# Moving nine gate chunks from the FoX loops to the sliding-window loops, and interleaving the prelude, in a fp32 hybrid attention layer

## The reference

```python
h = rmsnorm(x, norm_mix_pre)
z = h @ w_in   # FoX q,k,v (8 heads x 64) | forget logits (8) | SWA q (8x64), k, v (2x64) | gates g_fox, g_swa (1024 each)
logf = log_sigmoid(fa + fox_f_bias); cum = cumsum(logf)
# FoX: softmax(q.k/8 + cum_t - cum_s, causal) @ v
# SWA: chunks of 64, window of 3 chunks, relative bias, a sink per head, 4 query heads for one key head
y = sigmoid(g_fox) * (o_fox @ w_proj_fox) + sigmoid(g_swa) * (o_swa @ w_proj_swa)
x = x + rmsnorm(y @ w_o)
x = x + rmsnorm(conv_ffn(rmsnorm(x)))
```

## Time and profile before

| | |
|---|---|
| median of 3 runs | 1807.31 us (1806.53 to 1807.37) |
| the profiled execution, its time | 1807.58 us |
| its span, first to last instruction | 1805.8 us |
| TensorE busy | 1632.6 us (90%), 9375 products |
| VectorE, GpSimd, ScalarE busy | 992.1, 577.5, 430.7 us |
| mean granted TensorE clock | 0.961 of 2.4 GHz |

### The profile page before, as it was taken

How to read it: one execution, slowest core, us unless ns; L and a number is a source line. 1 busy time by engine, 2 the same in 40 slices (tenths; PEclk the granted TensorE clock), 3 DMA queues, 4 the chain that set the end, 5 groups by cost and what they waited for, 6 DMA issues and landing times.

```text
span 1805.8 us, 24441 instructions
## 1 busy us (share of the span) xinstructions
PE 1632.6 (90%) x9375; PEld 1512.7 (84%) x9375; DVE 992.1 (55%) x1874; ACT 430.7 (24%) x913; POOL 577.5 (32%) x312
## 2 busy tenths in 40 slices
PE   2779999999888977777699999999999999999996
PEld 2679999998877976766688799999999999999995
DVE  3645665657743258484944456455454554454456
ACT  4113342434521125352232211001001011011012
POOL 3242132222111330100813244334324324434442
PEclk9989999999988988897899999999999999999999
DMA  5342222222133420002543111101111112111115
GB/s 153 36 107 65 70 80 60 76 68 63 37 101 111 156 64 22 27 24 74 183 153 106 65 48 47 47 27 55 46 35 58 46 35 58 46 35 49 44 46 97
DMA packets 129615, 122.89 MB, mean 68 GB/s; under 512 B 7453, under 2 KB 116377, under 8 KB 129537
## 3 DMA queue, kind: packets, MB, share of 16 engines
q1 hardware_dynamic: 92468, 67.29, 13.0%
q10 hardware_dynamic: 35869, 50.22, 9.1%
q0 software_dynamic: 1200, 4.33, 1.4%
HBM read 94.00 MB, written 27.92 MB: 68 GB/s over the span
## 4 chain that ended last, share of the span: by engine, by line
PE 82%; DVE 13%; DMA 2%; issue 1%; ACT 1%; POOL 1%; SPq 0%; ACTq 0%; POOLq 0%; DVEq 0%
PE bank L643 17%; PE bank L644 17%; PE bank L645 17%; PE bank L649 6%; PE bank L651 6%; PE bank L650 6%; PE bank L675 5%; PE bank L787 2%; DVE m L1905 1%; DVE kl L1585 1%; DVE ssb L1658 1%; PE bank L758 1%; DMA raw<-in_w_in 1%; DVE ssb L1642 1%; PE bank L757 1%
## 5 line engine op out<-in xcount | busy, mean ns | idle before, releaser
L541 POOL TENSOR_TENSOR ring_h<-raw,att 128x1024 fp32r<-128x1024 f32 x108 | 208.2, 1928 | 1073.1 <-PE bank L645 844.8
L643 PE MATMUL bank<-m_h,ring_h 128*128 128x352 f32 x1056 | 340.7, 323 | 0.7 <-DVE m_l L1479 0.7
L644 PE MATMUL bank<-m_l,ring_h 128*128 128x352 f32 x1056 | 338.6, 321 | 0.0
L645 PE MATMUL bank<-m_h,ring_l 128*128 128x352 f32 x1056 | 338.4, 320 | 0.0
L643 PE MATMUL bank<-ht_h,ring_h 128*128 128x352 f32 x840 | 281.8, 336 | 11.1 <-DVE kt L1550 10.4
L542 POOL TENSOR_TENSOR ring_l<-raw,ring_h 128x1024 fp32r<-128x1024 f32 x108 | 287.9, 2666 | 8.5
L644 PE MATMUL bank<-ht_l,ring_h 128*128 128x352 f32 x840 | 275.6, 328 | 0.0
L645 PE MATMUL bank<-ht_h,ring_l 128*128 128x352 f32 x840 | 275.5, 328 | 0.0
L643 PEld LDWEIGHTS bank<-m_h,ring_h 128*128 128x128 f32 x1056 | 198.1, 188 | 1.2 <-DVE m_l L1479 0.8
L644 PEld LDWEIGHTS bank<-m_l,ring_h 128*128 128x128 f32 x1056 | 198.4, 188 | 0.3
L645 PEld LDWEIGHTS bank<-m_h,ring_l 128*128 128x128 f32 x1056 | 198.0, 188 | 0.0
(11 more groups left out here) (281 smaller groups left out, 2692.1 us busy)
## 6 DMA issues: line engine op xcount, KB each, us to landing
raw<-in_w_up SPq DMA_DIRECT2D x44, 512.0 KB, 4.0
raw<-in_w_in SPq DMA_DIRECT2D x35, 512.0 KB, 3.9
raw<-in_w_down SPq DMA_DIRECT2D x22, 512.0 KB, 3.6
d_gate<-gst ACTq DMA_DIRECT2D x48, 176.0 KB, 1.9
gm<-d_gate ACTq DMA_DIRECT2D x8, 528.0 KB, 4.3
d_mfox<-mst ACTq DMA_DIRECT2D x8, 528.0 KB, 2.9
gm<-d_gate ACTq DMA_DIRECT2D x24, 176.0 KB, 2.5
gm<-d_mfox ACTq DMA_DIRECT2D x24, 176.0 KB, 3.2
```

The costliest lines, as they stand in the source:

```text
L541: order.link(nc.gpsimd.tensor_tensor(high, src, zero.to_broadcast(list(src.shape)), ALU.add))
L643: nc.tensor.matmul(out, wh, xh, start=start, stop=False)
L644: nc.tensor.matmul(out, wh, xl, start=False, stop=False)
L645: return nc.tensor.matmul(out, wl, xh, start=False, stop=stop)
```

## The change

It makes no product more or less. It does this:

- **Slabs.** Pairs 0 to 2 have two gate slabs instead of three (15 fillers), the last pair three as before; the first SWA loop has gates 10 to 12 (nine whole chunks, one at each of steps 1 to 9), the second gates 13 and 14 (six, steps 2 to 7), where each had one slab in halves.
- **Prelude.** SP loads slab 0 after the third tile of x and slab 1 after the sixth, and takes over the 16 small loads. GpSimd makes four row scales before slab 0, and the others between slabs. ScalarE takes the highs of tile t - 4 behind the square of tile t. TensorE makes half a chunk after each tile from tile 3 on, the first chunk of `f`, `fk` and `fv` (order `early`). VectorE copies chunks between the operations of the forget chain. Pair 0 is prepared like the later pairs, head by head (`head_keys`, `head_queries`, `head_values`), its second head within the loop. The loads of `negc` go to ScalarE's queue.
- **SWA.** The step is scores, values, whole chunk, transposes; VectorE takes the lows of unit s - 2 before it scales unit s - 1; outputs go to `ot32` in fp32 and are split per pair of heads afterwards (`sw_out_high`, `out_low`).

```diff
 for pair in range(PAIRS):
     if pair == 0:
         SLABS += [("fk", 0), ("fv", 0), ("fq", 0)]
-    SLABS += [("gate", 3 * pair), ("gate", 3 * pair + 1)]
+    SLABS += [("gate", 2 * pair)]
     if pair + 1 < PAIRS:
-        SLABS += [("fk", pair + 1), ("fv", pair + 1), ("fq", pair + 1)]
-    SLABS += [("gate", 3 * pair + 2)]
...
+        SLABS += [("fk", pair + 1), ("fv", pair + 1), ("fq", pair + 1), ("gate", 2 * pair + 1)]
+    else:
+        SLABS += [("gate", 2 * pair + 1), ("gate", 2 * pair + 2)]
...
+    early = [(0, 0), (1, 0), (2, 0), (0, 1), (0, 2), (1, 1), (2, 1), (1, 2), (2, 2)]
...
-        if s <= 0:
-            return [0, 1] if (p == 0) == (s < 0) else []
-        return [s + 1] if s < 8 else ([9, 10] if s == 8 else [s + 2])
+        if p == 0 and s < 3:
+            return {-1: [0], 0: [1], 1: [2]}.get(s, [])
+        return [] if s in (-1, 3) else [s if s < 3 else s - 1]
+
+    def sw_fillers(g, s):
+
+        i = s - (1, 2)[g]
+        return [i] if 0 <= i < (9, 6)[g] else []
...
             for t in range(NT + 1):
                 sp.dma_start(xin[0:rows(t), t, :], tok_rows(xp, xs, t)).then_inc(x_in[t], 16)
...
+                if t == 2:
+                    slab_load(0)
+                if t == 5:
+                    slab_load(1)
...
+            pre_scales(range(0, 4))
             for n in range(S_FFN):
...
                     ring_split(n)
+                    if n < 3:
+                        pre_scales((range(4, 6), range(6, 8), range(8, 9))[n])
...
+            def dense_half(n, c, i):
+
+                q = position(n, c)
+                if i == 0:
+                    pe.wait_ge(slab_split, n + 1)
+                    pe.wait_ge(t_free, 6 * (c + 1))
+                    wait_bank_free(pe, q)
...
+                if t >= 3:
+                    dense_half((t - 3) // 2, 0, (t - 3) % 2)
...
+            for n, c in early[3:]:
+                dense_half(n, c, 0)
+                dense_half(n, c, 1)
...
                     if s < NT:
                         sw_scores(NT * g + s)
-                    if 2 <= s < 8:
-                        gate_half(SLAB["gate", 13 + g], s - 2)
                     if s >= 3:
                         sw_values(NT * g + s - 3)
+                    for i in sw_fillers(g, s):
+                        dense_chunk(SLAB["gate", (10, 13)[g]] + i // 3, i % 3)
                     if 1 <= s <= NT:
                         sw_transposes(NT * g + s - 1)
...
+            for t in range(NT + 5):
+                if t <= NT:
...
+                if t >= 4:
+                    pre_high(t - 4)
...
+            def sw_out_high(i):
+
+                act.wait_ge(pv_free, V_SW + NT * (i // 2 + 1))
+                copy(ot_h[:, i, 0:SEQ], ot32[:, i, 0:SEQ]).then_inc(ot_high, 1)
...
-                        order.catch_up()
-                        V.tensor_tensor(o3[0:HD], pv[:, :, 0, :], ot[:, :, 0, :], ALU.add)
-                        V.tensor_tensor(o3[HD:P], pv[:, :, 1, :], ot[:, :, 1, :], ALU.add).then_inc(pv_free, 1)
-                        dve.wait_ge(pv_free, v + 1)
                         dst = slice(P * qb, P * qb + P)
-                        link(V.tensor_copy(ot_h[:, 2 * g:2 * g + 2, dst], o3))
...
+                        V.tensor_tensor(ot32[0:HD, 2 * g:2 * g + 2, dst], pv[:, :, 0, :], ot[:, :, 0, :], ALU.add)
...
+            for i in (2, 3):
+                out_low(PAIRS + i)
```

More of the change, by code:

```diff
@@ L348, in program, with position, slab_end @@
         first_chunk.append(first_chunk[-1] + slab_chunks(n))
+    early = [(0, 0), (1, 0), (2, 0), (0, 1), (0, 2), (1, 1), (2, 1), (1, 2), (2, 2)]
+    def position(n, c):
+        return early.index((n, c)) if n < 3 else first_chunk[n] + c
+    def slab_end(n):
+        return max(position(n, c) for c in range(3)) + 1 if n < 3 else first_chunk[n + 1]
     owner = []
@@ L559, in mix_scales, with pre_scales @@
                 row_scale(rows(t), 12, 8)
+            def pre_scales(tiles):
+                for t in tiles:
+                    pool.wait_ge(pre_sq, t + 1)
+                    row_scale(rows(t), 27 + t, t)
+            pre_scales(range(0, 4))
             for n in range(S_FFN):
-                if n == 1:
-                    for t in range(NT + 1):
-                        pool.wait_ge(pre_sq, t + 1)
-                        row_scale(rows(t), 27 + t, t)
                 pool.wait_ge(raw_in[n % NRAW], 16 * (n // NRAW + 1))
@@ L679, in _ @@
             pe.wait_ge(ident_in, 16)
+            def dense_half(n, c, i):
[4 more added lines that the diff above has]
+                    wait_bank_free(pe, q)
+                for k in range(4 * i, 4 * i + 4):
+                    mm = three(bank[q % 3][:, 0:CH], ring_h[:, n % NSPL, k, :], ring_l[:, n % NSPL, k, :],
+                               ht_h[:, k, CH * c:CH * c + CH], ht_l[:, k, CH * c:CH * c + CH], k == 0, k == KT - 1)
+                if i:
+                    mm.then_inc(chunk_full, 1)
             for t in range(NT + 1):
@@ L705, in forget_rows @@
                     r = rows(t)
[L706 removed]
+                    mm = nc.tensor.transpose(bank[7][0:r, HEADS * t:HEADS * t + HEADS], lsr[:, 0, P * t:P * t + r],
                                              ident[0:HEADS, 0:HEADS])
@@ L821, in _ @@
                         prob_transposes(g - 1)
-            n = SLAB["gate", 12]
+            n = SLAB["gate", 9]
             dense_chunk(n, 0)
@@ L1504, in _ @@
             dve.wait_ge(misc_pe, MP_REL)
-            V.tensor_copy(relt[:, :], bank[2][0:HEADS, 0:RELS]).then_inc(misc_dve, 1)
-            for c in range(3):
-                dve.wait_ge(chunk_full, c + 1)
-                V.tensor_scalar(ls[:, 0, CH * c:CH * c + CH], bank[c][0:HEADS, 0:CH], smallf[0:HEADS, 0:1], None,
-                                ALU.add).then_inc(freed_dve, 1)
-            dve.wait_ge(freed_dve, 3)
-            V.scalar_tensor_tensor(ls[:, 1, :], ls[:, 0, :], -1.0, ls[:, 0, :], ALU.mult, ALU.max).then_inc(misc_dve, 1)
@@ L1567, in forget_rows, with keys_values_queries @@
                 V.tensor_copy(lfn[0:DEC, NT, :], bank[7][0:DEC, NT * HEADS:NT * HEADS + HEADS]).then_inc(misc_dve, 1)
-            def keys_values_queries(n, i0, count, q_out, first=False):
+            def keys_values_queries(n, i0, count, q_out):
                 for c in range(3):
@@ L1807, in _ @@
                                         ALU.subtract).then_inc(mx_ready, 1)
+                    if 2 <= s < NT + 2:
+                        u = NT * g + s - 2
+                        for k in range(SWB[u + 1] - SWB[u]):
+                            lows(T_SWA + 6 + SWB[u] + k, lambda b: (ptw_l[:, k, :], b[:, :], ptw_h[:, k, :]))
                     if 1 <= s <= NT:
@@ L1820, in _ @@
                         ins.then_inc(p_ready, 1)
-                    if 2 <= s < NT + 2:
-                        u = NT * g + s - 2
-                        for k in range(SWB[u + 1] - SWB[u]):
-                            lows(T_SWA + 6 + SWB[u] + k, lambda b: (ptw_l[:, k, :], b[:, :], ptw_h[:, k, :]))
                     if s >= 3:
```

311 lines of the change are left out of this document (167 added, 144 removed).

## The result

| | before | after |
|---|---|---|
| median of 4 runs | 1806.92 us (1805.09 to 1807.37) | 1749.67 us (1747.95 to 1750.28) |
| ratio, 95% interval | | 0.9684 (0.9672 to 0.9696) |
| span of the profiled execution | 1805.8 us | 1746.0 us |
| TensorE busy, products | 1632.6 us, 9375 | 1616.0 us (93%), 9375 |
| VectorE, GpSimd, ScalarE busy | 992.1, 577.5, 430.7 us | 982.8, 577.6, 434.3 us |

What follows compares the result with a forecast made beforehand. TensorE, busy 90% of the span, was taken as the bound, VectorE in the SWA loops. From 1805.8: prelude −43, FoX chunks −30.7, waits +14, SWA +5 gives 1751.1 us of span, forecast 1752.6 us, range 1738 to 1771.

Steps and rivals of the forecast that it cites:

- step five: Prelude's end: query copy, highs, lows and row staging run uncovered, 3 to 5 us idle, then a chunk at half clock.
- The start: Prelude: row scales before slab 0 and earlier highs bring tile 3's transpose to about 24.5 from 38.24, saving 13.7 us.
- 14 us come back: First three FoX pairs: four uncovered waits of 3 us, plus 2 for the clock, return of 30.7 saved; 8 to 25.
- the floor: FoX steps without a filler: each wait was put at 2 to 4 us, taken as 3.
- the item I set at nothing: FoX pair 0: head 1's new key, query and value halves lie under chunks; 6 us if that cover were gone.
- VectorE is the bound there: SWA loops: VectorE, busy 49.2 and 49.5 of 60.4 us each, was said to set their time.
- the forecast 9 us higher: SWA loops: by the skill's rule three more splits cost up to two full GpSimd instructions each, sum some 9 us higher.
- Rivals 1 and 2: Prelude gives 28, not 43 (1768 us, chance 0.15); GpSimd falls on VectorE wherever a chunk left (1773 us, chance 0.12).
- rival 3: Better everywhere: FoX waits 8, SWA 0, prelude 49; 1736 us, chance 0.10.
- Rival 4: SWA: chunk and VectorE's chain run one after the other, ScalarE a unit behind; +75, 1828 us, chance 0.02.

Runs made afterwards that it cites:

- experiment 9: Changed kernel with the old start: SP loads slabs 0 and 1 behind x, GpSimd splits slab 0 before the row scales; 1758.94 us.
- experiment 10: Changed kernel with VectorE's copies of the four early key and value chunks moved behind the forget chain's last operation; 1758.28 us.
- Experiment 2: Kernel before, with its old prelude, but with the nine chunks moved and the new SWA loops; 1785.27 us.
- experiment 1: Changed kernel with nine gate chunks put back into the FoX loops and halves again in the SWA loops; 1785.57 us.
- experiment 5: Changed kernel with the old SWA order around whole chunks: chunk ahead of values, scaling ahead of lows, outputs as before; 1766.77 us.
- experiment 6: Changed kernel with VectorE scaling unit s - 1 before it takes the lows of unit s - 2; 1748.45 us.
- experiment 11: Changed kernel with filler 2 per pair halved (pair 0 also filler 1), pair 0's value rows behind first scores, its second head's key highs before the loop; 1733.83 us.
- Experiment 12: experiment 11 with second SWA loop's chunks as halves over steps 1 to 9, last pair's halves one step earlier, first SWA outputs split later; 1728.26 us.
- experiment 7: Changed kernel with TensorE making the SWA values behind the whole chunk instead of ahead of it; 1814.84 us.

## Why the prediction was right, and where it was not

**Prelude: right step by step, 2.4 us too good.** Tile 3 was transposed at 25.5 (forecast 24.5), three chunks at 43.3 (46), the forget chain's end at 77.63 (77.5), scores at 96.43 (94). The miss is in step five: the 5.04 us of waiting were at the top of "3 to 5 us idle", and the third query chunk ran slow too (5.66 us, not 3.84). The start was given 13.7 us; tile 3 came 12.7 earlier, and experiment 9, which takes back 10.1 of them, moved the scores by 11.4 and the time by 9.3. The copies between the chain's operations are worth 8.6 (experiment 10), near the 10.4 of the earlier trace rows.

**FoX: the sum right, its parts not.** "14 us come back" was 12 for four waits of 3 and 2 for the clock. By the ledger 13.2 came back (280.65 against 298.1 - 30.7). Experiment 2 has 9.8 of it: 6.6 of waits at the four bare steps and 3.2 of other idle and slow time. The four waits of 1.6 to 1.7 us there, and two of four in the changed kernel, are less than the 2 that I gave as the floor. In steps 3 of pairs 1 and 2 a split did run beside them, but what it held was VectorE's next instruction (2.96 us instead of 1.22 at 208.39), for which no transposes waited. The other 3.5 us (280.65 against 277.2) are the item I set at nothing, the halves of pair 0's second head within the loop; some 2 of them are in the waits of 2.03 and 3.27. Two misses cancelled each other, so that the sum came out is in part luck. Moving the chunks alone is worth 21.0 us in the pairs.

**The last pair.** 4.7 us came from a place where the two kernels issue the same instructions. Behind the same wait of 3.44 us the granted clock was 0.50 in 439.06 to 444.90 and is 0.69 in 380.96 to 386.16: twelve products took 2.57 us instead of 3.82. Over the whole stretch TensorE made the same products in 200.6 us instead of 206.1 and was idle no less (32.6 and 31.8 us), so all of the gain is the clock's. In the thirteen kernels that leave this stretch alone it took 233.2 to 239.2 us. I had no term for that scatter, and the 4.7 us are luck in my total.

**SWA: the number near, its reason wrong.** The step that failed is "VectorE is the bound there", and from it the unit of 5.8 us that VectorE would need. As a sum of work it was true (0.18 us idle in before's unit), but the ring was as long. The change left VectorE idle time, and the unit stayed at 6.48 with half chunks (experiment 1): that is the length of a ring, not the load of an engine. Forecast unit 6.7, measured 6.61: TensorE's own work happens to be 0.13 us above the ring, so the right number was luck; with a ring of 8.4 it would have been 17 us off (experiment 5). Loops 61.3 and 61.4 (forecast 59.5 and 60), ahead of the second 3.4 us of wait instead of 2.25 (+1.2, forecast +3), at the end nothing (+1). In all it is +2.1 in this trace and +0.1 to +0.2 in six others, where I gave +5. I credited the order of lows and scaling, which does nothing (experiment 6), and passed over the values ahead of the chunk, which are worth 17 us or 65 by what stands beside them.

**Splits: right.** I counted 1.1 us each, on the ground that a whole chunk puts the split behind the scaling. In the changed kernel no scaling was held (277, 349 and 356 ns at least, median and most, against 2501 in the earlier trace rows); four statistics of the two loops were (0.81 to 1.54 us instead of 0.16), one of them this:

```profile
654.72 1.54 DVE L1874 TENSOR_TENSOR att<-att,smallf 128x4 f32<-128x4 f32 x1
```

It ended at 656.26, with GpSimd's instruction of 653.83 and 2.40 us, and TensorE waited 1.03. Behind the three others it waited 0.67, 1.04 and 4.13, the last at a step without a filler, where experiment 11, too, has a wait of 4.13. Experiment 12 moved the split, and the 4.7 us of the earlier trace rows came back. The rule in the Trainium skill, SBUF — State Buffer, section "SBUF: two separate sides" (the engine that comes second waits for a whole instruction), holds in both places; the forecast 9 us higher did not come, since it depends on which instruction is met. It goes the other way too: at 685.33 VectorE's lows of the outputs (1.23 us) and GpSimd's second split instruction start together, and the latter takes 3.48 us instead of some 2.4.

**Rivals.** Rivals 1 and 2 did not come: the first half chunk ran slow (3.87 us), the five others took 2.2. Of rival 3 the FoX waits (8; 8.6 measured) and the SWA loops (0; +0.1 to +2.1) nearly came, the prelude of 49 did not, and the prepared head and slow time made up the rest. Rival 4 priced a loop in which chunk and VectorE's chain follow each other at +75, and experiment 7 made one of +65. The likeness is chance: the rival's cause was ScalarE falling a unit behind, the cause there is the one buffer `ptw_h` with the values behind the chunk, while ScalarE is busy for only 75.7 of 219 us.

## What to carry to other kernels

When two engines wait for each other a little in every unit, neither is the bound: follow one buffer around (who must read it before it is written again) and keep the long filler out of that ring; then the filler is nearly free, 0.13 us for 1.92 us of products here. Take fillers from a stage that TensorE bounds and put them where it is idle (nine chunks put back cost 35.9 us, all of their products), leave half of one where the next stage needs cover, and look whether moving it also moves GpSimd's next split onto an instruction of VectorE.

## What the runs showed that I had not expected

One moved call cost 65 us: two orders that are each cheap (lows first, 1.2 us; values late with scaling first, some 17 us with before's outputs) are slower together than the kernel before. And the same instructions behind the same wait got a granted clock of 0.50 in one kernel and 0.69 in another; the stretch that holds them scattered by 6 us over thirteen kernels, so a term under some 5 us can't be read from one trace without looking at the clock of its rows.
